# Attention loop of a two-layer hybrid trunk: the sums of the two attentions exchange PSUM banks, the MLA pair goes last in its step, and the copy of the transposed differential probabilities goes between two maxima

## The reference, cut to what matters

```python
def _sdpa(q, k, v, scale):                                  # MLA
    s = jnp.einsum('bqhd,bkhd->bhqk', q, k).astype(F32) * scale
    p = jax.nn.softmax(s, axis=-1).astype(v.dtype)
    return jnp.einsum('bhqk,bkhd->bqhd', p, v)

def _diff_sdpa(q1, q2, k1, k2, v, scale, lam):              # differential
    p1 = jax.nn.softmax(jnp.einsum('bqhd,bkhd->bhqk', q1, k1).astype(F32) * scale, axis=-1)
    p2 = jax.nn.softmax(jnp.einsum('bqhd,bkhd->bhqk', q2, k2).astype(F32) * scale, axis=-1)
    return jnp.einsum('bhqk,bkhd->bqhd', (p1 - lam * p2).astype(v.dtype), v)
```

## Time and profile before

| | |
|---|---|
| median of 3 runs | 2948.03 us (2946.21 to 2948.14) |
| the profiled execution, its own time | 2947.06 us |
| its span in the trace | 2945.3 us |
| TensorE busy | 2846.3 us (97%) |
| VectorE busy | 1678.3 us (57%) |
| ScalarE busy | 881.7 us (30%) |
| mean granted TensorE clock | 0.99 |
| chain that ended last | PE 93%, DVE 3%, ACT 3% |
| attention loop, layer 0 | from 831.4 us to 983.8 us |
| attention loop, layer 1 | from 2368.2 us to 2490.1 us |

### The profile page before, as it was taken

How to read it: one execution, slowest core, us unless ns; L and a number is a source line. 1 busy time by engine, 2 the same in 40 slices (tenths; PEclk the granted TensorE clock), 3 DMA queues, 4 the chain that set the end, 5 groups by cost and what they waited for, 6 DMA issues and landing times.

```text
span 2945.3 us, 43839 instructions
## 1 busy us (share of the span) xinstructions
PE 2846.3 (97%) x16950; PEld 2433.6 (83%) x16950; DVE 1678.3 (57%) x3117; ACT 881.7 (30%) x1370; POOL 106.6 (4%) x82
## 2 busy tenths in 40 slices
PE   6999999999988999999999999999999988999998
PEld 4888888888756788888888888888888756898996
DVE  5876677733467578767776335443434476543443
ACT  4221122233256442211222321122233355422222
POOL 0000000043000000000000000000024000000000
PEclk8999999999999999999999999999999999999999
DMA  6444344322300134433442213221222200233232
GB/s 224 126 126 126 100 124 131 109 63 58 81 1 1 29 93 136 129 118 106 127 123 89 64 58 116 70 64 57 69 72 71 76 1 1 83 89 100 87 102 68
DMA packets 422759, 255.39 MB, mean 87 GB/s; under 512 B 26017, under 2 KB 418057, under 8 KB 422666
## 3 DMA queue, kind: packets, MB, share of 16 engines
q1 hardware_dynamic: 422160, 254.00, 28.9%
q10 hardware_dynamic: 506, 0.13, 0.0%
HBM read 252.01 MB, written 2.10 MB: 86 GB/s over the span
## 4 chain that ended last, share of the span: by engine, by line
PE 93%; DVE 3%; ACT 3%; issue 1%; DMA 0%; SPq 0%; DVEq 0%; ACTq 0%
PE pair L685 56%; PE pair L679 26%; PE pair L902 2%; PE pair L948 2%; ACT buf L1229 1%; PE pair L651 1%; PE pair L916 1%; PE pair L880 1%; PE pair L933 1%; DVE neg_max L1672 1%; PE pair L925 1%; PE pair L862 1%; DVE lo_w L1362 0%; PE pair L868 0%; PE pair L873 0%
## 5 line engine op out<-in xcount | busy, mean ns | idle before, releaser
L685 PE MATMUL pair<-n_hi,hi_w 128*128 128x260 f32 (+2 forms) x3456 | 846.8, 325 | 19.6 <-DVE n_lo L1401 13.5
L685 PE MATMUL pair<-n_lo,hi_w 128*128 128x256 f32 (+1 forms) x3456 | 844.2, 324 | 0.0
L685 PE MATMUL pair<-n_hi,lo_w 128*128 128x258 f32 (+2 forms) x3456 | 844.1, 325 | 0.0
L685 PEld LDWEIGHTS pair<-n_hi,hi_w 128*128 128x128 f32 x3456 | 531.6, 189 | 83.0 <-issue 11.0
L685 PEld LDWEIGHTS pair<-n_hi,lo_w 128*128 128x128 f32 x3456 | 536.1, 190 | 58.4
L685 PEld LDWEIGHTS pair<-n_lo,hi_w 128*128 128x128 f32 x3456 | 534.0, 189 | 54.9
L1362 DVE TENSOR_TENSOR lo_w<-raw_w,hi_w 128x1024 fp32r<-128x1024 f32 (+1 forms) x296 | 394.3, 1332 | 302.3 <-ACT hi_w L1028 301.5
L1028 ACT CAST hi_w<-raw_w 128x1024 fp32r<-128x1024 f32 (+1 forms) x296 | 328.8, 1111 | 653.2 <-PE pair L685 365.1
L1534 DVE SCALAR_TENSOR_TENSOR mod_acc<-mod_w,silu_c,mod_acc 128x256 f32<-128x256 f32 x896 | 364.6, 478 | 0.0
L1457 DVE TENSOR_TENSOR buf<-pair,rstd 128x512 f32<-128x512 f32 (+1 forms) x308 | 164.7, 570 | 309.1 <-PE pair L685 309.1
L679 PE MATMUL pair<-h_hi,hi_w 128*128 128x512 f32 x1232 | 338.8, 345 | 0.0
(11 more groups left out here) (186 smaller groups left out, 1981.4 us busy)
## 6 DMA issues: line engine op xcount, KB each, us to landing
raw_w<-in_ffn_w SPq DMA_DIRECT2D x176, 512.0 KB, 3.8
mod_w<-in_w_mod SPq DMA_DIRECT2D x64, 1024.0 KB, 5.1
raw_w<-in_ffn_w SPq DMA_DIRECT2D x64, 704.0 KB, 4.7
raw_w<-in_w_in SPq DMA_DIRECT2D x38, 512.0 KB, 3.9
raw_w<-in_w_out SPq DMA_DIRECT2D x16, 512.0 KB, 4.0
pro_scale<-in_w_mod SPq DMA_DIRECT2D x2, 2048.0 KB, 16.3
pro_shift<-in_w_mod SPq DMA_DIRECT2D x2, 2048.0 KB, 13.0
x_tok<-in_x SPq DMA_DIRECT2D x4, 512.0 KB, 5.6
```

The lines of the kernel that those rows point to most:

```text
L685: mm = pe.matmul(pair[s][:, a:a + m], wt[:, k * P:(k + 1) * P], src[:, of(k):of(k) + m], start=opens, stop=closes)
```

## The change

```diff
-            return pair[0][:, TOK:1024] if c < N_STEPS[L] - 1 else pair[2][:, P:3 * P]      # acc_mla
+            return pair[1][:, TOK:1024] if c < N_STEPS[L] - 1 else pair[2][:, P:3 * P]
-            return pair[1][:, TOK:TOK + P] if c < N_STEPS[L] - 1 else pair[2][:, 0:P]       # acc_diff
+            return pair[0][:, TOK:TOK + P] if c < N_STEPS[L] - 1 else pair[2][:, 0:P]
...
-                    pe.wait_ge(exp_done[0], st0 + c + 3)                                    # values_mla
+                    pe.wait_ge(exp_done[1], st0 + c + 3)
...
-                pe.matmul(acc[:, P:2 * P], inv_wide[(st0 + c) // 2 % 2], ident[:, :], start=True, stop=True)\
-                  .then_inc(pv_mla, 1)
+                for e in range(2):
+                    mm = pe.matmul(acc[MV * e:MV * (e + 1), P:2 * P],
+                                   inv_sum[:, slot(c - 1 + e, 2)].broadcast_to([P, MV]), ident[:, :], start=True, stop=True)
+                mm.then_inc(pv_mla, 1)
...
-                        pe.wait_ge(exp_done[1], st0 + c + 2)                                # values_diff
+                        pe.wait_ge(exp_done[0], st0 + c + 2)
...
                    if c < n_steps:
                        scores_mla(c)
-                    if c % 2 and c >= 3:
-                        values_mla(L, c - 2)
                     if c:
                         values_diff(c - 1)
                         transposes_mla(c - 1)
+                    if c % 2 and c >= 3:
+                        values_mla(L, c - 2)
...
+                def probabilities_mla(c):                                                   # ScalarE
+                    nk = steps[c][3]
+                    act.wait_ge(t_mla, st0 + c + 1)
+                    if st0 + c > 1:
+                        act.wait_ge(pv_mla, (st0 + c) // 2)
+                    act.copy(pt_m[c % 2][:, 0:nk], pair[3][:, 0:nk]).then_inc(pt_mla, 1)
...
-                    if c % 2 and c >= 3:
-                        turn_inverse(c - 2)
                     if c:
                         out_diff(c - 1)
-                        act.wait_ge(t_mla, st0 + c)
-                        if st0 + c > 2:
-                            act.wait_ge(pv_mla, (st0 + c - 1) // 2)
-                        act.copy(pt_m[(c - 1) % 2][:, 0:steps[c - 1][3]], pair[3][:, 0:steps[c - 1][3]]).then_inc(pt_mla, 1)
+                    if c and c % 2 == 0:
+                        probabilities_mla(c - 1)
                     if c < n_steps:
                         if c:
                             act.wait_ge(t_mla, st0 + c)
                         exponential(c, 2)
+                    if c % 2:
+                        if c >= 3:
+                            turn_inverse(c - 2)
+                        probabilities_mla(c - 1)
...
-                    dve.reciprocal(inv_wide[pairs % 2][:, e * MV:(e + 1) * MV],             # inverse_mla
-                                   exp_sum[:, slot(c, 2)].broadcast_to([P, MV])).then_inc(inv_mla, 1)
+                    dve.reciprocal(inv_sum[:, slot(c, 2)], exp_sum[:, slot(c, 2)]).then_inc(inv_mla, 1)
...
                     if c < n_steps:                                                         # VectorE
                         maxima(c, 0)
-                        maxima(c, 1)
-                    if c - 3 in pieces:
-                        low_mla(c - 3)
                     if c:
                         dve.wait_ge(t_diff, st0 + c)
                         if st0 + c > 1:
                             dve.wait_ge(pv_diff, st0 + c - 1)
                         dve.tensor_copy(pt_d[:, 0:steps[c - 1][3]], pair[3][:, 0:steps[c - 1][3]]).then_inc(pt_diff, 1)
+                    if c < n_steps:
+                        maxima(c, 1)
+                    if c:
                         inverse_mla(c - 1)
+                    if c - 3 in pieces:
+                        low_mla(c - 3)
```

More of the change, by code:

```diff
@@ L264, in build @@
         pt_d, squares, *pt_m = (proj[:, (T_DV + i) * TOK:(T_DV + i + 1) * TOK] for i in range(4))
-        inv_wide = [wk_n[:, i * 2 * MV:(i + 1) * 2 * MV] for i in range(2)]
         inv_rows = wk_n[:, 4 * MV:6 * MV]
@@ L1688, in inverse_mla @@
                 def inverse_mla(c):
-                    pairs, e = (st0 + c) // 2, c % 2
                     dve.wait_ge(exp_done[2], st0 + c + 1)
-                    if pairs > 1:
-                        dve.wait_ge(pv_mla, pairs - 1)
-                    dve.reciprocal(inv_wide[pairs % 2][:, e * MV:(e + 1) * MV],
-                                   exp_sum[:, slot(c, 2)].broadcast_to([P, MV])).then_inc(inv_mla, 1)
+                    if st0 + c > 3:
+                        dve.wait_ge(pv_mla, (st0 + c) // 2 - 1)
+                    dve.reciprocal(inv_sum[:, slot(c, 2)], exp_sum[:, slot(c, 2)]).then_inc(inv_mla, 1)
                 def scale_mla(c):
```

## The result

| | before | changed |
|---|---|---|
| median of the first 4 runs | 2947.12 us | 2923.27 us (2922.35 to 2926.13) |
| ratio, 95% interval | | 0.9922 (0.9906 to 0.9937) |
| profiled execution, own time | 2947.06 us | 2926.13 us |
| its span | 2945.3 us | 2924.4 us |
| all runs of this study | 2945.7 median, 44 runs, 2942.1 to 2949.0 | 2923.3 median, 14 runs, 2920.1 to 2928.1 |

The kernel is 0.8% faster. The forecast was 2929, and its range ended at 2926. (The 44 and 14 runs leave out the single executions of experiments 13 to 16.)

The account below looks back on a forecast made before the run. TensorE was taken as the bound, its differential values waiting for VectorE's copy. Gains in even, odd and short steps, less 0.9 us of losses, totalled 19.1 us: 2947.06 to 2928.0, 2929 on the median's scale, range 2926 to 2937.

Parts of the forecast that it names:

- The even step: Attention loop: 5.90 us with or without low part, from 7.44 or 6.76; exponential 0 last instead of the copy.
- The odd step: Attention loop: 7.53 us against 7.60, from 5.90, 1.31 for the pair and 0.32 for inverse and change to next scores.
- Rival C: Inverse's repeated-column loads overlap with nothing: 28 us lost, 19 won, 2957, chance 0.04; milder form 2939, chance 0.06.
- What is late next: Second maximum, exponential 1, combination and copies of MLA probabilities all finish in time, with slacks of 0.2 to 0.3 us.
- A: Rival: the next wait, for combination or MLA probabilities' copy, takes 2 to 7 us of the gain; 2931 to 2936; chance 0.18.
- The wait now: Differential values L948 stood ten times waiting for VectorE's copy L1722, up to 2.0 us for the weight load.
- The narrow inverse: VectorE's wide reciprocal, 0.46 us, becomes 0.18: worth nothing by itself where TensorE bounds, but it keeps a 0.3 slack.
- the change of shape: TensorE, odd steps: three tiling mode changes instead of four, about 0.15 us each; without that 7.68, sum 2.7 us smaller.
- The sum: All loop steps of both layers: 19.1 us less in total, from 2947.06 to 2928.0, 2929 on the median's scale.
- Short steps 10 and 22: Layer 0: the 0.84 us wait for the copy goes in each, 1.7 us together.
- Steps 8 and 20: Copy of the MLA probabilities comes behind a long pair, scores before it short: 0.25 us lost in each.
- how the numbers follow: Chances and range: forecast 0.66, likeliest 2929, up to 2937, down to 2926 because a run varies by 1.

Follow-up runs that it names:

- experiments 13 to 16: No edit, single profiled executions: 13 and 15 of the kernel before, 2945.30 and 2941.28 us; 14 and 16 of the changed kernel, 2924.96 and 2921.54 us.
- experiment 8: Changed kernel with the old inverse, written 64 columns wide and turned by one matmul over 128 rows: 2930.93 us, ratio to before 0.9955.
- experiment 13: Kernel before, unedited, its third profile, a single execution: 2945.30 us.
- Experiments 2 and 10: 2: kernel before with only the copy moved, 2967.10 us. 10: changed kernel with the MLA pair back ahead of the differential values, 2978.59 us, ratio to before 1.0113.
- Experiments 6 and 7: Unread filling matmuls: 6, kernel before, at step 0 of each layer and layer 0's steps 10 and 22, 2948.18 us; 7, changed kernel, step 0 only, 2925.85 us.
- experiment 2: Kernel before with only the copy of the transposed differential probabilities moved between the two maxima: 2967.10 us against 2944.76, ratio 1.0071.
- experiment 1: Changed kernel again, no edit: 2923.01 us against 2944.76, ratio 0.9926; its profiled execution 2920.14 us.
- experiment 9: Changed kernel a third time, no edit: 2924.71 us, ratio to before 0.9924; its profiled execution 2928.08 us.

## Why the prediction was wrong, by its own steps

**The even step**, 5.90: measured 5.88 in both kinds. The stall for the copy goes, exponential 0 is last. Right.

**The odd step**, 7.53: measured 7.56. The pair took 1.36 where 1.31 was reckoned, the four records of the inverse 0.32 as taken, in couples 0.11 apart (the last change of shape included). Rival C, slow loads of the repeated column, is out.

**What is late next**: no transposes waited in the full steps, so A did not come. It does hold in one place that the sum missed, step 2 of each layer with 6.02, 0.12 more than 5.90.

**The wait now** was misread in part. The ten waits for the copy are seven steps, since three of them stand both in the row of the weight loads (7) and in that of the matmuls (3). And in even steps without a low part it was exponential 1 that came last, as step 4 above shows. The new order removes both waits, so the step's length came out right.

**The narrow inverse** "worth nothing by itself where TensorE bounds": its half on VectorE, yes; the half on TensorE is worth 0.2 us in each odd step (experiment 8). The prediction had reckoned with 0.15 for it, under the change of shape.

**The sum**, 19.1: 19.8 by like steps. Short steps 10 and 22 gave 1.05 each, not 0.84. Steps 8 and 20 lost 0.18 each, where 0.25 was forecast. The last steps, priced at a loss of 0.2 each, gave 0.3 and 0.05. Steps 9 and 21 (0.08 lost each), 11 (0.15 lost) and 13 (0.10 won) were not priced.

**The step that failed** is in how the numbers follow: "a run varies by 1: down to 2926". It rests on three times that lay high and close together, and it puts changes of the clock at nothing: the granted clock is read for steps 2 to 14 of layer 1 alone ("all at full clock"), while the sum prices steps outside them too. A run of the kernel before varies from 2942.1 to 2949.0, one of the changed kernel from 2920.1 to 2928.1. The spread goes with the granted clock of the whole execution:

| granted clock | before, mean us (runs) | changed, mean us (runs) | difference |
|---|---|---|---|
| 0.989 | 2947.0 (9) | 2927.8 (2) | 19.3 |
| 0.990 | 2945.4 (22) | 2924.6 (6) | 20.8 |
| 0.991 | 2943.0 (7) | 2922.8 (3) | 20.2 |

So at a like clock the change is worth about 20 us, as the steps say. The forecast, 2929, is off by 5.7. Some 2.3 of this is its starting point: it was taken off 2947.06 and 2948.03, where 44 runs have their median at 2945.7. The sum's own error is 0.7. Of the 2.7 that are left the clock makes some 1.6: the changed kernel's 14 runs have a mean granted clock of 0.9905, the 40 of the kernel before that have it on record 0.9899, and in the table 0.001 goes with 2 to 3 us. About 1 us stays unexplained.

In the first pair of profiles one can see it step by step. Step 1, which the sum priced at 0.9 in each layer (right at full clock: 6.73 in experiment 13 to 5.85), gave 1.9 (7.77 to 5.85, and 8.10 to 6.20), and step 11 of layer 0 gave 0.8 where none was reckoned. In all three the kernel before stood at half clock in that one execution. Rows of it show it, here layer 0's step 1, with scores of 2.63 us where 1.56 is usual:

```profile
837.41 2.63 PE L902 MATMUL pair<-proj 64*128 64x512 f32 x8 [1.58 <-ACT buf L1229]
```

These rows were there to be read before the forecast. The other way, outside the loops the changed kernel's profiled execution took 1.5 us longer than the other's, so that its own gain, 20.9, lies below that of the medians.

**What stays open**: whether the changed kernel has fewer such stretches by nature. For it: behind step 1, three of the four profiles of the kernel before have one or two of them in the loops (at step 11, at 18, and twice at 22), worth 1.0 to 2.6 us, and none of the five of the changed kernel has any. Experiments 2 and 10 speak for a link too: with waits near 1.8 us in every other step the loops lost 10 and 12 us more than their steps at full clock explain. Against it: over the whole execution the nine profiles show as much half clock in the changed kernel (some 56 us) as before. Nine profiles are too few. Experiments 6 and 7 give no way to use it: with step 0 filled the time did not fall.

Also open is what the exchange of the banks is worth by itself. No run leaves out the exchange and keeps the rest. That it is needed is argued from experiment 2, where the copy stands in its new place, the banks are the old ones, and the values wait for exponential 1.

## What to carry to other kernels

When an instruction waits for several things, write down when each would be ready in the new order, and price the next one to come last. Moving the copy alone cost 22 us, and leaving out any one of three parts (copy, pair's place, ScalarE's order) gave back between 6 us and more than the whole gain. The full steps of a hand-made schedule like this one could be reckoned to 0.05 us from intervals between starts in one trace; the steps at its edges came out up to 0.5 us off. What could not be reckoned is the clock, so a range needs the spread of many runs, not the three at hand, and the granted clock of every step that the sum prices.

## What the runs showed of the hardware

TensorE stood at half its clock in stretches that moved between executions of one and the same program. Those in the loops stood behind holes in its work: 0.84 us (the wait for the copy in steps 10 and 22), 1.6 us (the waits of steps 0 and 18), 2.5 and 2.7 us (the entrances of the two loops). The same holes had no such stretch behind them in other executions. One stretch cost up to 1.5 us (a step of 8.93 instead of 7.44). The profiles with a mean granted clock of 0.992 (experiment 1, 2920.14) and 0.989 (experiment 9, 2928.08) lie 7.9 us apart at the same full steps, so the clock makes most of the 7 to 8 us by which equal runs differ.

The matmuls of the inverse on 64 columns with a stationary operand that repeats one column run at the pace of ordinary ones, 0.39 us for four records from the first start to the last end.

ScalarE, busy 65% of the two loops in the changed kernel (167.5 of 256.4 us), set the step when two copies changed places with the exponential (5.88 to 6.14 us).
